# GpSimd makes 20 of its 52 one-hot columns between the row gathers of the last early groups

## The reference, cut to what matters

```python
def peer_ffn(xn, wq, sub_keys, u_tab, v_tab):
    s = jnp.einsum('bshpd,hpnd->bshpn', q, sub_keys)      # 8 heads, 2 halves, 128 keys
    top_v, top_i = lax.top_k(s, 16)
    cand_v, cand_i = lax.top_k(cand, 16)                  # best 16 of the 16 x 16 sums
    experts = i1 * 128 + i2                               # 16 of 16384 experts per token and head
    gates = softmax(cand_v)
    act = gelu(einsum('td,tkd->tk', xb, u_tab[eb]))       # one dot product of 2048 per expert
    out = einsum('tk,tkd->td', gb * act, v_tab[eb])       # sum over 8 heads x 16 experts
```

## Time and profile before

| | us |
|---|---|
| median of 3 runs | 2805.58 |
| lowest, highest | 2804.15, 2809.61 |
| the profiled execution's own time | 2804.46 |
| its span, first to last instruction | 2802.7 |

### The profile page before, as it was taken

How to read it: one execution, slowest core, us unless ns; L and a number is a source line. 1 busy time by engine, 2 the same in 40 slices (tenths; PEclk the granted TensorE clock), 3 DMA queues, 4 the chain that set the end, 5 groups by cost and what they waited for, 6 DMA issues and landing times. The chain is left out here.

```text
span 2802.7 us, 39708 instructions
## 1 busy us (share of the span) xinstructions
PE 2296.4 (82%) x14809; PEld 2093.5 (75%) x14809; DVE 2090.2 (75%) x2718; ACT 1235.8 (44%) x1872; POOL 700.1 (25%) x394
## 2 busy tenths in 40 slices
PE   7999999999999999999899100004369999999998
PEld 6989999999999888899799100003258878888886
DVE  6785456666645755654459999999976889999996
ACT  4554544444444443443354000139954434444443
POOL 0000000000000100010003786887861233334330
PEclk9999999999999999999999655555589999999999
DMA  7544565555475565564459997999938899999995
GB/s 210 151 144 121 170 183 166 151 151 163 140 217 169 170 190 189 176 199 136 143 195 334 371 391 309 397 399 390 399 135 294 329 409 422 422 422 422 422 414 198
DMA packets 325176, 729.37 MB, mean 260 GB/s; under 512 B 23256, under 2 KB 265136, under 8 KB 267072
## 3 DMA queue, kind: packets, MB, share of 16 engines
q1 hardware_dynamic: 277648, 386.18, 41.4%
q0 software_dynamic: 46912, 340.81, 30.4%
q10 hardware_dynamic: 496, 0.84, 0.1%
HBM read 725.66 MB, written 2.10 MB: 260 GB/s over the span
## 5 line engine op out<-in xcount | busy, mean ns | idle before, releaser
L385 DVE TENSOR_TENSOR b_w_both<-b_raw,b_w_both 128x1024 fp32r<-128x1024 f32 x464 | 569.2, 1244 | 466.2 <-ACT b_w_both L380 465.0
L380 ACT ACTIVATE b_w_both<-b_raw 128x1024 fp32r<-128x1024 f32 x464 | 484.7, 1057 | 586.2 <-PE bank L403 393.2
L403 PE MATMUL bank<-b_act_both,b_w_both 128*128 128x256 f32 x4224 | 518.3, 285 | 7.5 <-DVE b_w_both L385 7.5
L403 PEld LDWEIGHTS bank<-b_act_both,b_w_both 128*128 128x128 f32 x4224 | 512.2, 193 | 10.4 <-DVE b_w_both L385 5.5
L753 POOL DMA_INDIRECT b_u_ring<-in_peer_u,b_idx_all x192 | 416.6, 2170 | 153.0 <-DVE b_dots L2061 76.2
L1187 ACT ACTIVATE b_v_hi<-b_v_raw 128x1024 fp32r<-128x1024 f32 x256 | 271.9, 1062 | 401.9 <-PE bank L1618 313.3
L2061 DVE CUSTOM_DVE_ANT_0 b_u_ring<-b_u_ring,b_xnN 128x2048 f32<-128x2048 f32 x192 | 436.5, 2278 | 0.0
L403 PE MATMUL bank<-b_att_both,b_w_both 128*128 128x256 f32 x3072 | 376.3, 285 | 0.0
L403 PEld LDWEIGHTS bank<-b_att_both,b_w_both 128*128 128x128 f32 x3072 | 372.8, 193 | 0.9 <-issue 0.7
L2113 DVE TENSOR_TENSOR b_v_lo<-b_v_raw,b_v_hi 128x1024 fp32r<-128x1024 f32 x256 | 309.3, 1220 | 65.7 <-ACT b_v_hi L1187 65.4
L1618 PE MATMUL bank<-b_v_hi,b_e_hi 128*128 128x512 f32 x1024 | 317.0, 391 | 0.0
(11 more groups left out here) (327 smaller groups left out, 2886.3 us busy)
## 6 DMA issues: line engine op xcount, KB each, us to landing
b_v_raw<-in_peer_v SPq DMA_DIRECT2D x128, 1024.0 KB, 9.1
b_raw<-in_w_in SPq DMA_DIRECT2D x208, 512.0 KB, 4.1
b_raw<-in_w_proj_dsa SPq DMA_DIRECT2D x32, 512.0 KB, 3.8
b_raw<-in_w_proj_gla SPq DMA_DIRECT2D x32, 512.0 KB, 3.5
b_raw<-in_w_xk SPq DMA_DIRECT2D x32, 512.0 KB, 4.4
b_raw<-in_w_out SPq DMA_DIRECT2D x32, 512.0 KB, 4.5
b_raw<-in_w_xv SPq DMA_DIRECT2D x32, 512.0 KB, 4.6
b_raw<-in_w_xq SPq DMA_DIRECT2D x32, 512.0 KB, 3.7
```

Of the source, the lines that this page charges most:

```text
L380: act.activation(w_hi[:, q], raw[:, UQ * c + q], ACT.Copy).then_inc(w_high, 1)
L385: dve.tensor_tensor(w_lo[:, q], raw[:, UQ * c + q], w_hi[:, q].bitcast(F32), ALU.subtract).then_inc(w_split, 1)
L403: mm = pe.matmul(proj[c][:, n], lhs, rhs, start=(q == 0 and n == 0 and k == 0 and t == 0), stop=(q == UQ - 1 and k == UK - 1 and t == 2), ...
```

## The change

GpSimd still makes the columns of octets 3 to 15. Of these, the 20 columns of octets 3 to 7 are now made one at a time inside `gather_rows` of groups 9, 10 and 11: after every second gather (k odd) one column, that is 8 in group 9, 8 in group 10 and 4 in group 11, after gathers 145, 147 and so on to 183. Before the first of them GpSimd waits for the turned tables of indices and for 8 units to be spread. The last 8 gathers (184 to 191) have nothing between them. `pool_cols` then makes the other 32 columns, octets 8 to 15, under the same waits as before.

```diff
+COLS_AMID = 5
+AMID_FROM = EARLY - 3
...
+    def make_oct_col(eng, o, m):
+
+        at = P + UNIT * o + m
+        return eng.tensor_scalar(oct_cols(o)[:, m], consts[:, C_IOTA:], turned[:, 1, at:at + 1], None, ALU.is_equal)
+
     def make_oct_cols(eng, o, done):
 
         for m in range(UNIT):
-            at = P + UNIT * o + m
-            ins = eng.tensor_scalar(oct_cols(o)[:, m], consts[:, C_IOTA:], turned[:, 1, at:at + 1], None, ALU.is_equal)
+            ins = make_oct_col(eng, o, m)
         ins.then_inc(sem(done), 1)
...
+                if g >= AMID_FROM and k % 2:
+                    col_amid((g - AMID_FROM) * PTOP // 2 + k // 2)
+
+        def col_amid(n):
+
+            o, m = COLS_BY_VECTOR + n // UNIT, n % UNIT
+            if n == 0:
+                pool.wait_ge(sem("tables_turned"), 3)
+                pool.wait_ge(sem("unit_spread"), MADE_AHEAD)
+            if n < COLS_AMID * UNIT:
+                ins = make_oct_col(pool, o, m)
+                if m == UNIT - 1:
+                    ins.then_inc(sem("cols_by_pool"), 1)
 
         def pool_cols():
 
-            pool.wait_ge(sem("tables_turned"), 3)
-            pool.wait_ge(sem("unit_spread"), MADE_AHEAD)
             pool.wait_ge(sem("dotted"), EARLY * PTOP - 4)
-            for o in range(COLS_BY_VECTOR, OCTETS):
+            for o in range(COLS_BY_VECTOR + COLS_AMID, OCTETS):
```

## The result

The changed kernel takes 2823.52 us in the median (2819.90 to 2830.83, 6 runs); the kernel before, beside it, 2807.68 us (2804.15 to 2811.88, 6 runs). The ratio is 1.0054, 95% interval 1.0041 to 1.0067: the change costs about 16 us. The profiled executions have spans of 2822.0 and 2802.7 us.

The account below looks back on a forecast made before the run. VectorE's dots were taken to bound the gathering, with GpSimd passing one instruction per dot. Stalls of 19.7 us plus 0.5 for longer dots minus 2.6 in the tail gave +17.6 us on 2805.6, so 2823 us, range 2816 to 2831.

Parts of the forecast that it names:

- The bound: Groups 9 to 11: VectorE's dots, busy 126.00 of 126.00 us, set the pace; a delay should reach the end nearly whole.
- One instruction per dot: Gathering: GpSimd gets one instruction through per dot, at the boundary, so each column costs one; dot period 2.63 us.
- The tail: Behind the gathers: 27 instead of 47 columns remain after the last dot, octets follow at 1.24 us, gain 2.6 us.
- The loss in the gathering: Groups 9 to 11: 20 columns cost 19.7 us of stalls, bounds 12.8 to 25.5, plus 0.5 for longer dots.
- The cover: Gathering: rows lie ready 9.3 us before their dots, covering 4 columns (10.5 us); one more is taken as free.
- The landing: Gathered rows: landing time, 8.7 us in the median, falls towards the shortest, 5.6 us.
- The payback: Gathering, from the fifth column on: a stall lets two extra instructions through, so one of 2.63 us for two columns.
- What dots pay: Dots beside a column take 0.10 to 0.17 us more; 0.5 us in all, upper bound 2.4.
- A: Rival: columns fit without missing a boundary, only the tail's gain is left, 2803 us; chance 0.11.
- B: Rival: GpSimd wins the port, each of 20 dots starts 0.60 us late, +9.4 us, 2815; chance 0.06.
- C: Rival: stalls pay nothing back, each column after the cover costs a full dot period, +39.5 us, 2845; chance 0.09.
- The sum and the time: Whole kernel: 19.7 + 0.5 - 2.6 = +17.6 us, forecast median 2823 us; chance 0.74.

Follow-up runs that it names:

- e2: Changed kernel, but the 20 columns amid the gathers are extras 32 elements wide and all 52 are made behind them: 2819.16 us, ratio 1.0042 to before.
- e3: Changed kernel, but GpSimd fills the places of the 20 columns amid the gathers with zeros, reading nothing: 2804.46 us, ratio 0.9991 to before.
- e5: Kernel before, but each dot replaced by a one-input sum of the gathered row, without the product or its write-back: 2803.73 us, ratio 0.9995 to before.
- e6: Changed kernel, but each dot replaced by a one-input sum of the gathered row, without the product or its write-back: 2802.38 us, ratio 0.9983 to before.
- e1: Changed kernel, but the 20 columns amid the gathers are extras and all 52 are made again behind them: 2825.14 us, ratio 1.0066 to before.
- e10: Changed kernel, but only 12 columns (octets 3 to 5) amid the gathers, one after each fourth gather: 2818.89 us, ratio 1.0033 to before.
- e4: Changed kernel, but only the 4 columns of octet 3 amid the gathers, early in group 9, and 48 behind: 2808.66 us, ratio 1.0005 to before.
- e9: Changed kernel, but only 4 columns amid the gathers, placed late, after gathers 185, 187, 189 and 191: 2807.86 us, ratio 1.0003 to before.
- e8: Kernel before without the wait for dot 187, so GpSimd's columns start right behind the last gather: 2805.18 us, ratio 0.9999 to before.

## Why the prediction was right, point by point

- **The bound.** VectorE's dots set the pace and a delay there arrives whole: shown. The values take 722.5 us before and 722.6 after.
- **One instruction per dot.** Shown by e2 (the size of the instruction matters little), e3 (no reading, no cost) and e5 with e6 (a sum in place of the dot, no cost). These leave the neighbouring explanations without support: neither the length of GpSimd's list nor a full queue of transfers holds the gathers at 2.3 us, as the DMA engines are as full in e5 (404 GB/s from 1903 to 2029 us) with gathers of 0.97 us. The rule of the Trainium skill that I cited ("SBUF — State Buffer", "Who interferes with whom") names two conditions, two SBUF inputs on VectorE's side and a read on GpSimd's. For the columns the traces agree: 2.4 us beside dots and 0.63 beside sums, and 0.22 for a fill beside dots. The gathers (2.3 and 0.97 us) fit it if their reading of the row numbers from SBUF counts as such a read, which no run here separates. Either way the engines, which I said meet only at semaphores, also meet within their instructions.
- **The tail.** I had a gain of 2.6 us, and 2.5 was measured, with octets at 1.24 us to the end. The other runs put the gain between 0.7 and 2.5 us, so the closeness is partly luck. One detail was wrong: I let GpSimd make five of the remaining columns before the last dot's end. They begin at octet 8, which waits for the last routing, and so GpSimd stood 10.5 us, the second wait shown above, and began at 2068.9, after the last dot. It was still done before TensorE needed it. All octets from 8 on stand behind this wait.
- **The loss in the gathering.** I had 20.2 us (19.7 of stalls and 0.5 of longer dots), and the profile has 20.1. An agreement to 0.1 us is luck: the stalls were 3.0 us shorter, VectorE's own slowdown (next point) made up for it, and e1, with the same work up to the last gather, lost 16.7 in all. What was right is the mechanism: a cover that is used up first, then stalls that pay part back. Two terms were mis-sized. The cover: it carries about four columns. The fifth, which I took as free, brings the first stall, 1.51 us before dot 154 in the changed kernel and 1.80 us before dot 164 in e10; in e1 a stall of 0.59 us stands already behind the fourth. The landing, which I let fall towards 5.6 us, fell only from 8.8 us in the median of the stretch to 7.7 (after, 18 of the 48 recorded) and 7.6 (e1, all). The payback: I counted 2.63 us of stall for two columns, 1.3 each, and 16.7 us for the 16 columns from the fifth on is 1.0. Missing altogether was a second use of the cover: it takes up the irregularities of all gathers behind. Spent early in group 9, it is missing for some 40 rows, and that is nearly all of the 4.2 us of e4; spent at the end, nobody needs it (0.2 us, e9). The runs give 4.2, 11.8, 20.1 and 39.0 us for 4, 12, 20 and 40 instructions, about 1.0 us for each, with 0.8 in e1. That is a handy line but not one mechanism: the first four pay through the rows behind them, the others through stalls of their own. That the small stalls of e4 come from irregular gathers and transfers is read from its trace and from e9; no run made them regular.
- **What dots pay.** The 48 dots of the stretch sum to 111.1 us and to 109.3 before, +1.8. I had 0.5. Together with 16.7 us of idle time that makes 18.5 of the 20.1; the other 1.6 us lie between the dots, where VectorE runs its short instructions, and the sum had no term for them.
- **The rivals.** A (the columns fit) fell with the first row of waits. B (the dots pay the whole column) would have put 12 us into dots, which lost 1.8. C (no payback) would have cost 42 us; the timeline above shows the payback, a column and a gather in one stall.
- **The sum and the time.** +17.6 us was forecast; the spans differ by 19.3, of which 17.6 are the two pieces (20.1 - 2.5) and the rest lies ahead of gather 144, where nothing was changed. The runs give +15.8 between the medians, or 11.5 to 18.8 us by the interval. That the forecast of 2823 meets the median of 2823.5 owes something to the later runs of the kernel before, which lie 2 us higher than those that I started from.

## What to carry to other kernels

An engine's idle share is no room: ask per instruction what it waits for within its own record, and count the moments at which it gets through. Beside the long dots of this kernel a GpSimd column that began amid a dot lasted until past the dot's end, also with a quarter of the work, and each one placed ahead of many gathers cost 0.7 to 1.05 us. Put such work behind the last GpSimd step that VectorE depends on: there four columns waited just as long and cost 0.4 us (e8). And time that data lie ready is not free to spend: it is also what absorbs irregular gathers and transfers, and the earlier it is spent, the more rows run without it (4.2 us in e4, 0.2 in e9).

## What the runs showed of the hardware

- A GpSimd fill of 128 x 128 float32, which reads nothing, took 0.22 us amid dots with two SBUF inputs, and moved neither a dot nor a gather: gathers kept a mean of 2.3 us and VectorE never idled (e3).
- A 128 x 32 `tensor_scalar` on GpSimd took 1.9 to 2.6 us amid the dots, hardly less than the 2.4 us of 128 x 128 (e2).
- Beside one-input sums of the same length (2.27 us), which write one column, gathers took 0.97 us, not 2.3, with the same traffic (e5): what looked like a busy GpSimd was waiting inside the instruction.
- In the changed kernel a gather right behind a column begins 0.17 us after it, and one right behind a gather 0.30 us.
- A column and a dot that overlap share the delay unevenly: columns beside dots took 2.4 us in place of 0.6, while the dots beside them took 0.1 to 0.2 us more.
